# One attention loop, three queues in a new order: scores two tiles ahead, copies first, exponentials before scaling

## What is computed

```python
def one_block(i):                                    # 128 queries, for every head
    s_c = einsum(qb, k_c) * scale                    # compressed keys (31)
    p_c = masked_softmax(s_c, c_end <= tpos)
    o_c = einsum(p_c, v_c)
    ...                                              # selected blocks
    s_s = einsum(qb, ks_g) * scale
    p_s = masked_softmax(s_s, m_s)
    o_s = einsum(p_s, vs_g)
    s_w = einsum(qb, kw) * scale                     # window
    p_w = masked_softmax(s_w, m_w)
    o_w = einsum(p_w, vw)
    return gb[0] * o_c + gb[1] * o_s + gb[2] * o_w
```

## Time and profile before

| | |
|---|---|
| runs | 2806.2, 2808.0, 2809.7 us; median 2808.0 |
| the profiled execution | 2809.1 us, span of the trace 2807.3 us |
| TensorE matmul busy | 2681.9 us, 96% of the span |
| VectorE, ScalarE, GpSimd busy | 56%, 38%, 42% |
| attention loop | 277.5 to 516.9 us, 239.4 us |

### The profile page before, as it was taken

How to read it: one execution, slowest core, us unless ns; L and a number is a source line. 1 busy time by engine, 2 the same in 40 slices (tenths; PEclk the granted TensorE clock), 3 DMA queues, 4 the chain that set the end, 5 groups by cost and what they waited for, 6 DMA issues and landing times.

```text
span 2807.3 us, 38071 instructions
## 1 busy us (share of the span) xinstructions
PE 2681.9 (96%) x13128; PEld 2198.0 (78%) x13128; DVE 1571.4 (56%) x2448; ACT 1055.5 (38%) x1826; POOL 1178.2 (42%) x592
## 2 busy tenths in 40 slices
PE   7999888899999999999999999999899999999998
PEld 6877666778888878878887788888687778888886
DVE  7996666564343376466665745545623447653364
ACT  4224777633222254443334411112525553211133
POOL 3432585244444444355423344444442214444443
PEclk9999999999999999999999999999999999999999
DMA  3242000133222232221102322222231112322222
GB/s 133 99 141 83 16 24 9 53 120 106 92 96 97 97 113 102 82 99 61 61 31 91 136 92 96 97 97 91 95 110 53 46 46 97 122 96 97 98 97 90
DMA packets 67460, 242.88 MB, mean 87 GB/s; under 512 B 7772, under 2 KB 10117, under 8 KB 66573
## 3 DMA queue, kind: packets, MB, share of 16 engines
q1 hardware_dynamic: 59760, 215.37, 22.6%
q10 hardware_dynamic: 7580, 25.91, 2.6%
HBM read 232.80 MB, written 6.35 MB: 85 GB/s over the span
## 4 chain that ended last, share of the span: by engine, by line
issue 47%; PE 34%; POOL 14%; DVE 2%; ACT 2%; POOLq 0%; DMA 0%; DVEq 0%; SPq 0%; ACTq 0%
POOL w_lo L442 12%; PE bank L2585 9%; PE bank L2587 9%; PE bank L2586 9%; PE bank L3133 2%; PE bank L3122 2%; POOL stat L469 1%; PE bank L2907 1%; POOL stat L466 1%; PE bank L2800 1%; PE bank L2894 0%; PE bank L2771 0%; ACT tmp L974 0%; DVE big L1925 0%; POOLq L446 0%
## 5 line engine op out<-in xcount | busy, mean ns | idle before, releaser
L442 POOL TENSOR_TENSOR w_lo<-raw,w_hi 128x1024 fp32r<-128x1024 f32 x398 | 972.4, 2443 | 1561.2 <-ACT w_hi L589 1439.9
L2585 PE MATMUL bank<-act,w_hi 128*128 128x512 f32 x3128 | 1259.0, 403 | 51.9 <-POOL w_lo L442 14.6
L2587 PE MATMUL bank<-act,w_lo 128*128 128x512 f32 x3128 | 1227.0, 392 | 0.0
L2586 PE MATMUL bank<-act,w_hi 128*128 128x512 f32 x3128 | 1226.6, 392 | 0.0
L589 ACT CAST w_hi<-raw 128x1024 fp32r<-128x1024 f32 x396 | 415.5, 1049 | 900.7 <-PE bank L2587 888.9
L2585 PEld LDWEIGHTS bank<-act,w_hi 128*128 128x128 f32 x3128 | 592.5, 189 | 199.7 <-issue 31.6
L2587 PEld LDWEIGHTS bank<-act,w_lo 128*128 128x128 f32 x3128 | 592.2, 189 | 126.9
L2586 PEld LDWEIGHTS bank<-act,w_hi 128*128 128x128 f32 x3128 | 592.9, 190 | 121.0 <-issue 5.5
L1685 DVE TENSOR_TENSOR X<-X,bank 128x512 f32 x56 | 38.5, 688 | 241.3 <-PE bank L2587 241.3
L2076 DVE CAST act<-tmp 128x512 f32 x64 | 142.4, 2225 | 10.0 <-DVE tmp L2072 5.2
L1837 DVE SCALAR_TENSOR_TENSOR bank<-big,cols,bank 128x512 f32<-128x512 f32 x174 | 117.0, 748 | 0.4
(11 more groups left out here) (427 smaller groups left out, 2962.5 us busy)
## 6 DMA issues: line engine op xcount, KB each, us to landing
raw<-in_w_dram SPq DMA_DIRECT2D x402, 512.0 KB, 3.4
act_f<-head_rows ACTq DMA_DIRECT2D x8, 768.0 KB, 4.2
proj_rows<-big ACTq DMA_DIRECT2D x4, 1024.0 KB
big<-proj_rows ACTq DMA_DIRECT2D x2, 2048.0 KB, 9.2
X<-in_x_dram SPq DMA_DIRECT2D x4, 512.0 KB, 6.1
act_f<-in_cw1k_dram ACTq DMA_DIRECT2D x4, 512.0 KB, 4.2
cst<-in_consts_dram ACTq DMA_DIRECT2D x2, 648.5 KB, 7.9
X<-big ACTq DMA_DIRECT2D x8, 128.0 KB, 3.4
```

The source lines that it names most:

```text
L442: pool.tensor_tensor(w_lo[:, u], raw[:, u].rearrange("p (k n) -> p k n", k=KT), w_hi[:, u].bitcast(F32), ALU.subtract).then_inc(w_lo_ready, 1)
L2585: pe.matmul(o, l_hi, r_hi, start=start, stop=False)
L2586: pe.matmul(o, l_hi, r_lo, start=False, stop=False)
L2587: return pe.matmul(o, l_lo, r_hi, start=False, stop=stop)
```

## The change

No instruction is added or taken away; three programs get another order within the round.

- TensorE computes the scores of tiles 0 and 1 ahead of the loop, and in round n those of tile n + 2, behind `values(n-3)` and `transposes(n-1)`. The compressed scores follow them.
- VectorE copies first (`keep_second_pt(n-2)`), then computes `row_factor(n)`, then the compressed shift, then `maxima(n+2)`, then the compressed sum.
- ScalarE computes `exps(n+1)` ahead of `scale_rows(n)`.

```diff
--- before.py
+++ after.py
@@ -1003,14 +1003,14 @@
                 for n in range(N + 2):
                     if n >= 2:
                         keep_pt(n - 2)
+                    if n + 1 < N:
+                        exps(n + 1)
                     if n < N:
                         scale_rows(n)
                     if n % 8 == 7 and n // 8 < 6:
                         keep_gate(n // 8 + 2, bank[1])
                     if n % 8 in (2, 4) and n // 8 + 1 < NH // 2:
                         compressed_exp(n // 8 * 2 + 2 + (n % 8 == 4))
-                    if n + 1 < N:
-                        exps(n + 1)
                     if 3 <= n < 7:
                         keys_high(2 + (n - 3) // 2, (n - 3) % 2)
                     if n % 8 == 2 and n // 8 < 6:
@@ -1971,23 +1971,24 @@
                 compressed_shift(0)
                 compressed_shift(1)
                 maxima(0)
+                maxima(1)
                 v.wait_ge(tok_kept, 5)
                 for q in range(TT):
                     link(v.tensor_scalar(V_TOK[:, 4, q, 0:NH], V_TOK[:, 4, q, 0:NH], const(1, "cmp_valid", 1, q), None, ALU.mult))
                 compressed_sum(0)
                 compressed_sum(1)
                 for n in range(N + 3):
+                    later = n // 8 + 1 < NH // 2
+                    if 2 <= n < N + 2:
+                        keep_second_pt(n - 2)
                     if n < N:
                         row_factor(n)
-                    if 2 <= n < N + 2:
-                        keep_second_pt(n - 2)
-                    if n + 1 < N:
-                        maxima(n + 1)
-                    if n // 8 + 1 < NH // 2:
-                        if n % 8 in (1, 3):
-                            compressed_shift(n // 8 * 2 + 2 + (n % 8 == 3))
-                        if n % 8 in (4, 6):
-                            compressed_sum(n // 8 * 2 + 2 + (n % 8 == 6))
+                    if later and n % 8 in (1, 3):
+                        compressed_shift(n // 8 * 2 + 2 + (n % 8 == 3))
+                    if n + 2 < N:
+                        maxima(n + 2)
+                    if later and n % 8 in (4, 6):
+                        compressed_sum(n // 8 * 2 + 2 + (n % 8 == 6))
                     if 4 <= n < 8:
                         keys_low(2 + (n - 4) // 2, n % 2)
                     if n >= 10 and (n - 10) % 8 == 0:
@@ -2923,17 +2924,18 @@
                 compressed_scores(0)
                 compressed_scores(1)
                 scores(0)
+                scores(1)
                 for n in range(N + 2):
                     if n < 6 * KT:
                         gate_filler(n)
-                    if n + 1 < N:
-                        scores(n + 1)
-                    if n % 8 in (0, 2) and n // 8 + 1 < NH // 2:
-                        compressed_scores(n // 8 * 2 + 2 + (n % 8 == 2))
                     if n % 2 and n >= 3:
                         values(n - 3)
                     if 1 <= n <= N:
                         transposes(n - 1)
+                    if n + 2 < N:
+                        scores(n + 2)
+                    if n % 8 in (0, 2) and n // 8 + 1 < NH // 2:
+                        compressed_scores(n // 8 * 2 + 2 + (n % 8 == 2))
                 c.add("act_read", 8)
 
 
```

## The result

The changed kernel takes 2855.5 us (2851.2 to 2858.3) against 2808.5 before in the same comparison: ratio 1.0166, interval 1.0150 to 1.0182, 47 us slower. The forecast had the direction, by 21 us, and put the time at 2829 with a range up to 2845, so the size is wrong.

A forecast was written before the change was run, and what follows sets the result against it. The prediction took a one-round circle of steps across engines, not busy shares, to bound the loop: 16.3 us for it plus 2, 1 and 2 for cast, port and clock, +21 on 2808.0, gave 2829 us, range 2814 to 2845.

The forecast's parts named there:

- The circle: One-round chain of copy, values, transposes, scores, maximum, sum or heads, next copy: 240.4 us in all, +16.3 us.
- TensorE's clock: Half-clock stretches after TensorE's idle time in the loop: taken at +2 us, bounds 0 to 14.
- the shared port: VectorE's two-input sums held up beside GpSimd in the loop: 0 to 10 us, taken at +1; the factor's delay hidden.
- the signs given for it: Maximum's idle time over 60 us, copy never behind transposes, factor's waits gone, 31 to 33 us per eight tiles.
- the 523.2: Predicted end in us of the last tile's maximum in the changed kernel: 282.8 plus 240.4.
- the 506.9: End in us of the last tile's maximum in the kernel before, 505.68 plus 1.21 from its profile.
- The rival with the clock (2841): Eight to ten half-clock stretches on the loop's chain cost +14 us instead of +2: 2841 us, chance 12%.
- The first eight tiles: Start of the loop: claimed to end where they did before.
- K2(n-2): VectorE's copy of the second branch's transposes of tile n-2.
- M(n+2): VectorE's maximum of the scores of tile n+2.
- The cast, +2: ScalarE's w_hi cast, one round in eight, may delay copy and values: 0 to 1 us a group, 2 in all.
- The decoupling pays: Rival: running further ahead ends the waits, the loop falls to some 26 us per eight tiles, 2783 us; chance 8%.

The follow-up runs named there:

- e2: Changed kernel with VectorE's copy of the transposes taken one tile earlier, ahead of the same round's maximum: 2805.5 us, ratio 0.9993.
- e3: Changed kernel with the scores of tile n+2 and the compressed scores moved ahead of values and transposes in TensorE's round: 2792.1 us, ratio 0.9943.
- e11: Kernel before with only TensorE's edit and the maximum two tiles ahead, row factor still first, ScalarE as before: 2894.2 us, ratio 1.0295.
- e6: Changed kernel with GpSimd's loop operations cut to one input, leaving out some tap sums and low halves of weights: 2842.6 us, ratio 1.0119.
- e5: Changed kernel with 204 more TensorE products: filler run twice in 36 rounds, six unread products in rounds 48 to 63: 2845.8 us, ratio 1.0124.
- e8: Changed kernel with both the 204 added TensorE products and GpSimd's loop operations cut to one input: 2841.3 us, ratio 1.0112.
- e7: Kernel before with GpSimd's loop operations cut to one input, some tap sums and low halves left out: 2796.4 us, ratio 0.9947.

## Why the prediction was right and wrong

The forecast was +21 us, measured were +47. The circle, its largest term, came out as priced. Two of the small terms fail: TensorE's clock, taken at +2 with a bound of 14, cost 19 to 23 us, and the shared port, taken at +1, cost 6 to 10.

**The bound and the circle: right.** The timeline shows the circle step by step, e2 and e3 each open it at another place and are rid of the whole 47 us, and e11 shows that this part alone costs more than the sum. Its price, 31.3 us per eight tiles, came out at 31.4 at full clock and without the holds. Of the signs given for it, these held: idle time of the maximum for scores 104 us (over 60), and the factor's waits for exponentials gone. VectorE's copy was to stand behind transposes "never"; it does three times (7.0 us), all behind the last maximum, which ends at 549.4 us, so not in a round of the circle. The pace of 31 to 33 us with and without fillers did not hold: the groups take 33.5 to 35.1 with them and 34.7 without, by the two terms below. VectorE's groups over the loop, answering to the earlier trace rows:

```profile
L1941 DVE COPY big<-bank 128x128 f32<-128x128 f32 (+3 forms) x64 | 30.8, 482 | 7.1 <-PE bank L2895 7.0
L1932 DVE TENSOR_TENSOR big<-big 128x2 f32<-128x2 f32 x64 | 30.0, 468 | 2.2
...
L1931 DVE RECIPROCAL big<-big 128x2 f32<-128x2 f32 x64 | 9.9, 154 | 0.1
```

**TensorE's clock: mis-sized.** The step took +2 us with a bound of 14. Over the loop 0.92 was granted, so 0.08 of 284.2, 22.7 us, was left out. In e6's third group such a stretch is paid in full (1.6 us of 1.65). Without fillers it is paid in part: 0.15 of 34.72, 5.2 us, was left out, and 3.1 us of it came back in e5 at full clock. If the port has 9 to 10 us, as the groups of e6 say, about 19 of the 22.7 fell to the clock; if all 22.7 did, 6 are left for the port. Their sum, 28.7, is measured; the split is no closer than that.

The error has three parts. First, I counted stretches of half clock from the group without fillers only and took the filler groups as before; the count in the loop went from four (0.97 granted) to some twelve. Second, 44%, TensorE's share of the circle, was too small a weight: behind an idle stretch the first work is TensorE's work on the circle, as e6's third group shows. Third, the four stretches of before were set off against the new ones, though the 523.2 was built from rows at full clock and the 506.9 was measured with those stretches in it: the whole loss had to be added, not the increase. The rival with the clock (2841) was the nearest of the four, and even it was too small. What calls a stretch isn't shown: the round above, with its 3.03 us of idle time, lies in a group of full clock.

**The first eight tiles: wrong.** They were to stay; they take about 4 us longer, because the half clock had begun at 275.4 us, just ahead of the loop, and lasted 10 us. The profiled e6 has a stretch of that length too, e5 and e8 haven't; it is part of the 22.7. It is not shown to be the change's doing: e2 and e3, which begin the loop in the same order, have none there, and e7, in the old order, has one.

**The shared port: wrong in its place.** That the factor's delay lies "between K2(n-2) and M(n+2)", where VectorE waits anyway, holds for most factors: L1932 loses 20 us in the changed kernel, and all holds together cost 6 to 10. But the step priced the hold by L469 (1.28 us) and not by GpSimd's 2.36 us operation L442, and it forgot the wait of scores 8k+5 for the shift, which the kernel's text shows and which stands behind the factor. Taken at +1, bound 10. The changed kernel's loop is 284.2 us; less 255.5 and 22.7 there are 6.0 left for it; by the groups of e6 against the changed kernel it is 2 to 3 us in each of four filler groups and nothing behind them, 9 to 10. So 6 to 10.

**The cast, +2:** never seen by itself. No run shows it; e6 meets a sum without it within 1 us.

**The sum.** 16.1 (255.5 less 239.4) + 28.7 for clock and port = 44.8 us for the loop. That it meets the 44.8 measured in the profiled executions says nothing, since the 28.7 is what was left over; the test of the 255.5 is e6. In the medians it is 47. That the loop's loss goes through "one to one" held within 3 us: spans 2849.4 less 2807.3 are 42.1, with the clock's other stretches differing between executions.

**The rivals.** "The decoupling pays" asks for scores that are ready when the maximum is due. That is e3, and there it does pay, 16 us, not the 25 of that rival. The prediction said that by the queues it can't happen here, and it didn't.

## What to carry to other kernels

Before a step is issued "further ahead", write down for each queue what stands in front of it and what is queued behind it; a step ahead in number may be later in its queue, and a copy whose input is ready must not stand behind a reduction whose input is late. Close the loop of such places once around and price it from rows; that gave this loop's pace at full clock to 0.1 us. Then price what the new idle stretches do to TensorE's clock, with nearly full weight where the chain has no slack, and remember that a path built from rows at full clock has none of that loss in it yet. Edits on different engines don't add: exponentials first costs 13 to 16 us or gains 20, depending on whether the maxima are a round further ahead.

## What the runs showed of the hardware

More work made a kernel faster: 204 added products in TensorE's idle time raised the granted clock over the loop from 0.92 to 0.98 and took 10 to 12 us off, while the same products cost the kernel before 22 us. Of four groups of eight rounds with the same products in e6, the one with 0.95 granted took 33.02 us, the three with 1.00 took 31.4. A two-column operation of VectorE with two SBUF inputs took 1.90 us beside a 2.36 us GpSimd operation and 1.24 beside a 1.29 us one; with GpSimd's operations down to one input, the 64 of them took 14.2 us in all instead of 30.0.
